# Third block of a fused transformer kernel: the token sums of x's squares enter the query norms once for all four heads, two weight splits stand ahead of the first update, and two turns stand one step later

## The reference, cut to what matters

```
# mixer: queries, keys, values, a compressed branch and gates from one product
h = rms_norm_2(x, norm_mix_g); z = h @ w_in
kc = rms_norm_2(compress_blocks(k_cmp, ...), k_norm_g[0])     # h1 = gelu(flat @ w1 + b1); h1 @ w2 + b2
g = sigmoid(gate_logits)
x = x + mixed @ w_out

# cross attention to the memory, 4 heads of 128
h = rms_norm_2(x, norm_mem_g)
q = rms_norm_2((h @ w_mq).reshape(B, T, 4, 128), q_g)
s = einsum('bthd,bmhd->bhtm', q, k) * 128 ** -0.5
x = x + (softmax(s) @ v) @ w_mo
```

## Time and profile before

| | us |
|---|---|
| three runs | 1308.6, 1314.57, 1317.26 (median 1314.57) |
| the profiled execution's own time | 1310.65 |
| its span in the trace | 1308.8 |
| TensorE busy | 1262.9 (96% of the span) |
| VectorE, ScalarE busy | 810.0 (62%), 670.6 (51%) |
| mean granted TensorE clock | 0.98 of full |

### The profile page before, as it was taken

One profiled execution on the slowest core, in us unless ns is written; L12 is line 12 of the kernel. 1 busy time (PEld: TensorE's weight loads), 2 busy tenths in 40 slices (PEclk: granted clock), 3 DMA queues, 4 the chain that ended last, 5 costly groups with the idle time before them and its releaser, 6 DMA issues.

```text
span 1308.8 us, 23587 instructions
## 1 busy us (share of the span) xinstructions
PE 1262.9 (96%) x10309; PEld 1232.0 (94%) x10309; DVE 810.0 (62%) x922; ACT 670.6 (51%) x960; POOL 91.9 (7%) x65
## 2 busy tenths in 40 slices
PE   3999999999999999999999999999899999999998
PEld 2999999989999999999888999999799998999998
DVE  5478547666664477854766766457777754666542
ACT  4466546455543446654545554345566543555432
POOL 3000001010000000001101000002101100100000
PEclk8999999999999999999999999999989997999999
DMA  5644553336655543454333666656442440366552
GB/s 180 221 133 130 179 165 123 108 115 215 205 195 195 167 132 106 136 179 161 116 108 116 211 208 194 194 175 189 124 130 65 149 142 16 117 213 204 198 191 95
DMA packets 195573, 202.92 MB, mean 155 GB/s; under 512 B 5716, under 2 KB 191847, under 8 KB 195471
## 3 DMA queue, kind: packets, MB, share of 16 engines
q1 hardware_dynamic: 192704, 194.82, 46.8%
q0 software_dynamic: 2464, 5.99, 1.5%
q10 hardware_dynamic: 303, 0.61, 0.2%
HBM read 200.33 MB, written 3.16 MB: 155 GB/s over the span
## 4 chain that ended last, share of the span: by engine, by line
PE 87%; DVE 4%; ACT 4%; DMA 2%; issue 2%; POOL 1%; SPq 0%; DVEq 0%; ACTq 0%
PE bank L574 14%; PE bank L576 14%; PE bank L575 14%; PE bank L2315 7%; PE bank L2319 7%; PE bank L2317 7%; PE bank L617 2%; PE bank L619 2%; PE bank L625 2%; PE bank L2232 2%; ACT w_hi L524 2%; PE bank L2216 2%; DVE w_lo L534 1%; PE bank L2158 1%; POOL sumsq L764 1%
## 5 line engine op out<-in xcount | busy, mean ns | idle before, releaser
L534 DVE TENSOR_TENSOR w_lo<-raw,w_hi 128x2048 fp32r<-128x2048 f32 (+7 forms) x210 | 424.7, 2031 | 332.8 <-ACT w_hi L524 332.5
L524 ACT ACTIVATE w_hi<-raw 128x2048 fp32r<-128x2048 f32 (+7 forms) x210 | 355.3, 1704 | 350.3 <-PE bank L2319 131.1
L574 PE MATMUL bank<-act_hi,w_hi 128*128 128x256 f32 (+1 forms) x1104 | 309.7, 281 | 0.0
L576 PE MATMUL bank<-act_hi,w_lo 128*128 128x256 f32 (+1 forms) x1104 | 306.9, 278 | 0.0
L575 PE MATMUL bank<-act_lo,w_hi 128*128 128x256 f32 (+1 forms) x1104 | 306.8, 278 | 0.0
L2315 PE MATMUL bank<-h_hi,w_hi 128*128 128x256 f32 x768 | 212.5, 277 | 0.0
L2319 PE MATMUL bank<-h_hi,w_lo 128*128 128x256 f32 x768 | 212.3, 276 | 0.0
L2317 PE MATMUL bank<-h_lo,w_hi 128*128 128x256 f32 x768 | 212.3, 276 | 0.0
L575 PEld LDWEIGHTS bank<-act_lo,w_hi 128*128 128x128 f32 (+1 forms) x1104 | 208.1, 188 | 0.4
L574 PEld LDWEIGHTS bank<-act_hi,w_hi 128*128 128x128 f32 (+1 forms) x1104 | 207.5, 188 | 0.9 <-issue 0.3
L576 PEld LDWEIGHTS bank<-act_hi,w_lo 128*128 128x128 f32 (+1 forms) x1104 | 207.5, 188 | 0.1
(11 more groups left out here) (379 smaller groups left out, 2146.6 us busy)
## 6 DMA issues: line engine op xcount, KB each, us to landing
raw<-in_w_up_dram SPq DMA_DIRECT2D x32, 1024.0 KB, 5.4
raw<-in_w_down_dram SPq DMA_DIRECT2D x32, 1024.0 KB, 5.1
raw<-in_w_ff_dram SPq DMA_DIRECT2D x32, 1024.0 KB, 5.4
raw<-in_w_in_dram SPq DMA_DIRECT2D x23, 1024.0 KB, 5.4
raw<-in_w_xk_dram SPq DMA_DIRECT2D x8, 1024.0 KB, 5.2
raw<-in_w_xv_dram SPq DMA_DIRECT2D x8, 1024.0 KB, 5.1
raw<-in_w_mix_out_dram SPq DMA_DIRECT2D x8, 1024.0 KB, 5.2
raw<-in_w_xq_dram SPq DMA_DIRECT2D x8, 1024.0 KB, 5.2
```

The source lines that it names most:

```text
L524: ins = act.activation(d, r, ACT.Copy)
L534: ins = dve.tensor_tensor(d, r, h.bitcast(F32), ALU.subtract)
L574: pe.matmul(o, stat_hi, mov_hi, start=first, stop=False)
L576: return pe.matmul(o, stat_lo, mov_hi, start=False, stop=last)
```

## The change

Four edits, all in the third block.

1. A new step `("hq", 6)` takes the place of `("hs", 6)` and `("hs", 7)`. It puts all eight columns into bank hs6: first x's squares, one product for each source and token half with four equal columns of the constant as the moving operand, so that each product adds to the four heads' columns at once (8 products in place of 32), then the eight sums of the heads' squares. Only these wait for `hs_square`. One root of eight columns and one reciprocal take the place of two of four; the two copies over the tokens stay.
2. `keep_clock` ahead of it makes two products instead of three.
3. ScalarE splits slabs 22 and 23 ahead of the first update and slab 24 ahead of the second, instead of 22, 23 and 24 ahead of the first, second and third.
4. `("cht", 0)` stands after slab 7, and `("gt", 0)` after `("scores", 4)`; banks 4 and 5, and 7 and 0, change places with them.

```diff
-WARM_2 = {("pair", 0): ("y0", 4), ("hs", 6): ("hs6", 3), ("hb", 6): ("scores12", 3), ...
+WARM_2 = {("pair", 0): ("y0", 4), ("hq", 6): ("hs6", 2), ("hb", 6): ("scores12", 3), ...
-     ("slab", 5), ("hb", 0), ("hb", 1), ("slab", 6), ("hs", 2), ("cht", 0), ("slab", 7), ("hb", 2), ("slab", 8),
+     ("slab", 5), ("hb", 0), ("hb", 1), ("slab", 6), ("hs", 2), ("slab", 7), ("cht", 0), ("hb", 2), ("slab", 8),
...
-        part_128, eps_sq_128 = small[:, 13:14], small[:, 14:15]
+        part_128, eps_sq_128 = row_sum[:, 40:44], small[:, 14:15]
...
-                      src_ready=updated(0, [[22], [23], [24], []]))
+                      src_ready=updated(0, [[22, 23], [24], [], []]))
...
-            head_root(6, 4, 1.0, eps_sq_128)
-            head_root(7, 4, 1.0, eps_sq_128)
+            head_root(6, 8, 1.0, eps_sq_128)
...
+            dve.wait_ge(once["hs_root"], 7)
+            then_next(dve.reciprocal(head_inv[0], head_inv[0]))
             for n in range(2):
-                head_inverse(6 + n)
+                dve.tensor_copy(head_sq[:, n, :].rearrange("p (w c) -> p w c", w=4),
+                                head_inv[0][:, 4 * n:4 * n + 4].unsqueeze(2).broadcast_to([P, 4, P])).then_inc(once["hs_rstd"], 1)
...
+            def query_sums(_):
+
+                b = open_bank(pe, DEPTH, "hs6")
+                open_bank(pe, DEPTH, "hs7")
+                pe.wait_ge(sig["sumsq"], value("sumsq", DEPTH, 4))
+                pe.wait_ge(sig["square"], value("square", DEPTH, 8))
+                pe.wait_ge(once["part_128"], 2)
+                for i in range(TI):
+                    for m, (src, a) in enumerate((src, a) for src in (sumsq, sq_next) for a in range(2)):
+                        t = T * a + P * i
+                        pe.matmul(b[:, i:8:TI], src[:, t:t + P], part_128, start=i == 0 and m == 0, stop=False,
+                                  skip_group_check=True)
+                for j in range(8):
+                    if j % 4 == 0:
+                        pe.wait_ge(once["hs_square"], 7 + j // 4)
+                    ins = pe.matmul(b[:, j:j + 1], head_sq[:, j // 4, P * (j % 4):P * (j % 4) + P], ones[:, 0:1],
+                                    start=False, stop=True, skip_group_check=True)
```

More of the change, by code:

```diff
@@ L140 @@
         ("pair", 32): ("up0", 3), }
-WARM_2 = {("pair", 0): ("y0", 4), ("hs", 6): ("hs6", 3), ("hb", 6): ("scores12", 3), ("scores", 12): ("scores12", 3),
+WARM_2 = {("pair", 0): ("y0", 4), ("hq", 6): ("hs6", 2), ("hb", 6): ("scores12", 3), ("scores", 12): ("scores12", 3),
           ("slab", 25): ("mo0", 2)}
@@ L145 @@
     [("pair", 0), ("stat", 0), ("slab", 2), ("slab", 3), ("slab", 4), ("hs", 0), ("hs", 1), ("sgw", 0), ("sgw", 1),
-     ("slab", 5), ("hb", 0), ("hb", 1), ("slab", 6), ("hs", 2), ("cht", 0), ("slab", 7), ("hb", 2), ("slab", 8),
+     ("slab", 5), ("hb", 0), ("hb", 1), ("slab", 6), ("hs", 2), ("slab", 7), ("cht", 0), ("hb", 2), ("slab", 8),
      ("scores", 0), ("scores", 1), ("scores", 2), ("cht", 1), ("scores", 3), ("slab", 9), ("turn", 0), ("turn", 1),
-     ("slab", 10), ("gt", 0), ("scores", 4), ("pv", 0), ("scores", 5), ("pv", 1), ("turn", 2), ("turn", 3), ("slab", 11),
+     ("slab", 10), ("scores", 4), ("gt", 0), ("pv", 0), ("scores", 5), ("pv", 1), ("turn", 2), ("turn", 3), ("slab", 11),
      ("pv", 2), ("pv", 3), ("turn", 4), ("turn", 5), ("hs", 3), ("slab", 12), ("pv", 4), ("pv", 5), ("scores", 6),
@@ L154 @@
      ("pv", 11), ("hb", 5), ("ot", 0), ("ot", 1), ("slab", 18), ("half", 19), ("ot", 2), ("ot", 3), ("half", 20),
-     ("rest", 19), ("rest", 20), ("slab", 21), ("slab", 22), ("pair", 23), ("hs", 6), ("hs", 7), ("hb", 6), ("hb", 7)]
+     ("rest", 19), ("rest", 20), ("slab", 21), ("slab", 22), ("pair", 23), ("hq", 6), ("hb", 6), ("hb", 7)]
     + [("scores", u) for u in range(12, 16)] + [("turn", 12), ("turn", 13), ("pv", 12), ("turn", 14), ("pv", 13),
@@ L214, in bank_uses_2 @@
             uses += slab_banks_2(n)
+        elif kind == "hq":
+            uses += [("hs6", "hs_done", 7), ("hs7", "hs_done", 8)]
         elif kind == "stat":
@@ L2371, in head_sums @@
                 w = over.shape[1]
[L2372 to L2381, removed]
                 for j in range(4):
                     ins = pe.matmul(b[:, w * j:w * j + w], head_sq[:, n % 2, P * j:P * j + P], over, start=True, stop=True)
+                ins.then_inc(once["hs_mm"], 1)
+            def query_sums(_):
[14 more added lines that the diff above has]
+                                    start=False, stop=True, skip_group_check=True)
                 ins.then_inc(once["hs_mm"], 1)
@@ L2614, in pair_2 @@
                 slab_pair(pe, DEPTH, s, names, {0: 0, 23: 16, 27: 24}[s])
-            steps_2 = {"slab": slab_2, "pair": pair_2, "stat": stat_2, "gt": turn_gates, "half": half_2, "rest": rest_2, "hs": head_sums, "hb": head_spread, "sgw": turn_token_weights, "cht": turn_hidden, "mem": turn_memory,
+            steps_2 = {"slab": slab_2, "pair": pair_2, "stat": stat_2, "gt": turn_gates, "half": half_2, "rest": rest_2, "hq": query_sums, "hs": head_sums, "hb": head_spread, "sgw": turn_token_weights, "cht": turn_hidden, "mem": turn_memory,
                        "vturn": turn_compressed_values, "cscores": compressed_scores, "cturn": turn_compressed,
```

## The result

| | kernel before | changed kernel |
|---|---|---|
| median, us | 1314.02 (1308.6 to 1317.26, 4 runs) | 1295.63 (1293.16 to 1299.16, 4 runs) |
| span of the profiled execution, us | 1308.8 | 1291.4 |
| mean granted clock | 0.98 | 0.99 |

The ratio is 0.986, 95% interval 0.984 to 0.9879: 18.4 us faster. In the two profiled executions the spans differ by 17.4 us.

The account below looks back on a forecast made before the run. TensorE, busy for 96% of the span, was taken to bound the kernel. Terms -12.3 - 4.6 + 1.8 - 0.9 = -16.0 us took the median 1314.57 to 1298.6, given as 1298 us; range 1291 to 1309.

Parts of the forecast that it names:

- first update: Around pair 23: earlier splits remove 2.92 us of TensorE idle time and 1.75 of half-clock stretch, 4.6 us gained.
- gates' turn: At the gates: the fifth scores fill 1.31 us of idle time and the values' product starts earlier, 0.9 us gained.
- What bounds the kernel: Whole kernel: TensorE is busy for 96% of the span; its idle time or lower clock moves the end.
- Query sums: From pair 23's end to the spreads: fewer narrow passes and fillers take 5.71 us instead of 17.99, 12.3 gained.
- The price by the Trainium skill: Query sums: a 107 ns weight load independent of the clock makes 48 passes worth 5.1 us, 1304 us in total.
- first turn: Compression's turn behind slab 7: VectorE's split of slab 8 queues behind the polynomial, slab 8 comes 1.8 us later.
- the clock does better: Attention behind the gates, 952 to 956 us: full clock instead of 0.50 wins 2 to 3.5 us, 1295 us; chance 0.14.
- the first rival: New sums or gap ahead of slab 8: the clock still falls once or twice, say 1302 us; chance 0.22.
- Split order brings nothing: Around pair 23: slab 25's load slows slab 24's, so the new split order gains nothing, 1303 us; chance 0.07.
- shared products dearer: Query sums: four columns with a stride of two cost 1.7 us or more, 1300 us; chance 0.05.
- The slower one: From the sums to slab 25: TensorE stays at 1.2 GHz, 1316 us, or 1327.5 if also before the gates; chance 0.04.

Follow-up runs that it names:

- e1: Kernel before with only the new query sums and the shorter filler ahead of them: ratio 0.9901 to the kernel before, -13.0 us.
- e12: Kernel before with three 256-column fillers ahead of every column of the old query sums but the first: ratio 1.003 to the kernel before.
- e10: Changed kernel with VectorE's split of slab 8 ahead of the compression's polynomial and two fillers between the two kinds of query sums: 1293.73 us.
- e7: Kernel before with a 256-column filler ahead of every second column of the old query sums, first left out, three in all: ratio 1.0027.
- e2: Kernel before with only the splits of slabs 23 and 24 moved ahead: ratio 0.9978 to the kernel before, -2.9 us.
- e3: Kernel before with only the compression's turn put behind slab 7: ratio 1.0009 to the kernel before, +1.2 us.
- e8: Changed kernel with its two fillers moved from ahead of the query sums to between x's squares and the heads' squares: 1297.5 us.
- e4: Kernel before with only the gates' turn put behind the fifth scores: ratio 0.9965 to the kernel before, -4.6 us.
- e11: Kernel before, order unchanged, with two 256-column fillers in the idle time ahead of the gates' turn: ratio 0.9984 to the kernel before.
- e5: Changed kernel with the compression's turn back ahead of slab 7: 1295.26 us, ratio 0.9834 to the kernel before.
- e6: Changed kernel with VectorE's split of slab 8 ahead of the compression's polynomial: 1293.87 us, ratio 0.9821 to the kernel before.

## Why the prediction was right

1298 us was forecast and 1295.6 measured, 16.0 us of gain and 18.4. The mechanisms came as described, but that the totals lie so close is in part luck: the first update alone brought 1.7 us less than its term, and the gates' turn 3.7 more. By its steps:

- *What bounds the kernel.* Right: all that moved the end was TensorE's idle time and TensorE's clock.
- *Query sums, -12.3.* Right: e1 gave -13.0, way C on average 20.5 - 8.8 = 11.7. That the clock had a part, some 7 of the 12.3, is shown by e12. That four columns cost no more than one was a choice and proved right (1.68 us for 16 passes of either in e10). The cover of the splits of slabs 26 and 27 held: they end at 1081.99, the first exponential begins at 1084.32 and had waited for VectorE's maximum.
- *The price by the Trainium skill.* The Trainium skill, "TensorE: Matmul & The Clock Gate", section "LDWEIGHTS (loading the stationary operand)", would have given 1304 us by a load of 107 ns whatever the clock. The narrow passes of e12 agree (111 ns at full clock), those of e7 at half clock don't (213), and the time went by the trace.
- *First update, -4.6.* The mechanism was right to within 0.4 us for each start, counted from the end of slab 20: no idle time, full clock, from the split of slab 22 to the end of pair 23 4.7 us less (29.69 to 24.95). The load of slab 25 did no harm: slab 24's landed in 5.0 us, as before. The timing of e2 gives -2.9 (-4.6 to -1.1), less than forecast though just within its interval. Its one trace doesn't show the missing 1.7 in the old sums (19.86 us as before); it lost 1.3 at the first turn, ahead of the edit, where other traces differ in the same way. What the traces do show is that the clock's part isn't always there: from the end of the turns of `("ot", 3)` to the end of pair 23 six traces of the old order take 35.3 to 35.5 us, but e3, whose clock didn't fall behind the idle time, 34.25, and the seven of the new order 30.7 to 31.1. On average this is 4.4 us. Whether the rest of the difference to e2's timing is chance stays open.
- *First turn, +1.8.* The wait came as computed (2.4 us on VectorE, 2.2 us on TensorE). On the time e3 gave +1.2, too little to tell from nothing. The prediction allowed for one half-clock stretch of 1.75 us; in e3 and e8 there are two, 3.0 us together (14.7 against 11.7), one of them ahead of the wait. And the old order has such a fall too, of 1.3, in five of eight traces, which I had not seen in the one trace that I had.
- *Gates' turn, -0.9.* This is the mis-sized term. The earlier start is there (0.8 us for 0.86), but e4 gave -4.6 (-6.3 to -2.9), and the longer way B 74.4 - 71.5 = 2.9. The prediction had the rest as a rival of its own, "the clock does better", and should have put it into the term: the stretch at 0.50 behind this idle time stood in the earlier trace rows. In the changed kernel's own trace that stretch is still there, and e11, which filled the idle time, didn't win the longer way; why the new order loses less to the clock stays open.
- *Rivals.* The clock fell once around the changed kernel's sums, among the fillers and spreads, as the first rival said, and the spreads took 1.5 us more, as priced; the gates' turn outweighed it. "Split order brings nothing" and "shared products dearer" are refuted by the traces. The slower one didn't come: from the end of the spreads to slab 25 it is 15.40 us in the changed kernel, where the clock stays at 1.00, against 16.17 before. In e5, e6, e8 and e10 a fall lies in it and it takes 15.9 to 16.2, so the six fillers don't always protect it.

## What to carry over

A stretch in which TensorE never idles can still run at half clock, as the old sums did: read the granted clock beside the busy share. Before calling a fall of the clock avoided, follow the trace to a later common point; here it often only moved. Sums over several outputs with the same source belong into one product with as many moving columns; here 40 became 16 at no higher price each. Moving a step to fill a wait can open another, if something is queued behind that step on another engine: VectorE's split of slab 8 is the example, and with it moved ahead and the fillers put between the sums the kernel ran at 1293.7 us, against 1296.7 for the changed kernel on the same chip, a difference within the scatter.

## What was not expected of the hardware

A few fillers didn't hold the clock and many did: with one 256-column product for 20 narrow passes it fell as before (e7), with three for ten it stayed at 2.4 GHz for 20 us (e12). And the same code meets the clock at different places. The sixteen spreads took 1.87, 2.50, 2.96, 3.27 and 3.30 us in five traces with the old sums, yet way C took only two values, 19.86 and 21.5, and the new sums two as well, 7.51 and 9.16: some 1.65 us apart both times. A single profile shows one draw of this. Such draws are not all of the scatter of 5 us and more in the times of one kernel: `("hs", 2)`, ahead of every edit, starts between 927.0 (the changed kernel) and 933.75 us (e6) in the fourteen traces. Why was not tried.
